# Inputs laid out by feature on the host, and index queries in five interleaved parts

## The reference

```python
def dsa_mixer(x, cos, sin, w_in, w_o):
    proj = x @ w_in
    q, k, v, iq, ik, iw = jnp.split(proj, A_SPLITS, axis=-1)
    ...
    s = jnp.einsum('bqhd,bsd->bqhs', iq_b, ik) * IDX_DIM ** -0.5
    score = jnp.einsum('bqh,bqhs->bqs', iw_b, jax.nn.relu(s))
    _, sel = lax.top_k(score, top_k)
...
    x = layer_norm_2(DEEPNORM_ALPHA * x + swiglu_ffn(x, ffn_w_in[i], ffn_w_down[i]), ...)
    x = x + jax.nn.sigmoid(x @ ple_w_gate[i]) * (p[i] @ ple_w_proj[i])
```

## Time and profile before

| | us |
|---|---|
| median of 3 runs | 1242.28 |
| lowest and highest run | 1242.15 and 1244.17 |
| span of the profiled execution | 1239.5 |
| PE busy in it | 1229.5 |
| DVE busy | 853.1 |
| ACT busy | 589.4 |

### The profile page before, as it was taken

How to read it: one execution, slowest core, us unless ns; L and a number is a source line. 1 busy time by engine, 2 the same in 40 slices (tenths; PEclk the granted TensorE clock), 3 DMA queues, 4 the chain that set the end, 5 groups by cost and what they waited for, 6 DMA issues and landing times.

```text
span 1239.5 us, 18755 instructions
## 1 busy us (share of the span) xinstructions
PE 1229.5 (99%) x7999; PEld 1050.9 (85%) x7999; DVE 853.1 (69%) x919; ACT 589.4 (48%) x712; POOL 94.9 (8%) x226
## 2 busy tenths in 40 slices
PE   9999999999999999999999999999999999999998
PEld 8888888888888888888988888888898888888887
DVE  6887776665775776666776676668587666766675
ACT  5774444334754544334654444345472544444434
POOL 5441000001000200000101000001000100000000
PEclk9999999999999999999999999999999999999999
DMA  8425665655633755654615656555564347655642
GB/s 282 170 69 166 209 197 181 199 187 156 221 115 129 266 183 191 202 175 157 222 60 182 216 181 203 180 194 204 180 191 158 103 150 237 200 186 188 200 141 101
DMA packets 127234, 221.03 MB, mean 178 GB/s; under 512 B 7048, under 2 KB 91296, under 8 KB 127152
## 3 DMA queue, kind: packets, MB, share of 16 engines
q1 hardware_dynamic: 124128, 209.83, 51.0%
q0 software_dynamic: 3024, 10.01, 2.6%
HBM read 218.77 MB, written 1.05 MB: 177 GB/s over the span
## 4 chain that ended last, share of the span: by engine, by line
PE 93%; DVE 3%; ACT 2%; DMA 1%; POOL 1%; issue 1%; SPq 0%; POOLq 0%; DVEq 0%
PE ps L794 20%; PE ps L622 18%; PE ps L796 10%; PE ps L599 10%; PE ps L600 10%; PE ps L601 10%; PE ps L762 4%; PE ps L810 2%; PE ps L706 2%; DVE wlo L1870 1%; PE ps L1034 1%; PE ps L981 1%; DMA raw<-in_ffn_w_in 1%; PE ps L1149 1%; ACT whi L1421 1%
## 5 line engine op out<-in xcount | busy, mean ns | idle before, releaser
L1870 DVE TENSOR_TENSOR wlo<-raw,whi 128x2048 fp32r<-128x2048 f32 (+3 forms) x203 | 452.1, 2241 | 174.6 <-ACT whi L1421 173.4
L1421 ACT ACTIVATE whi<-raw 128x2048 fp32r<-128x2048 f32 (+3 forms) x203 | 376.8, 1869 | 73.0 <-DMA raw<-in_hgrn_w_in 21.7
L794 PE MATMUL ps<-xhl,whi 128*128 128x512 f32 x1088 | 271.8, 392 | 0.0
L794 PEld LDWEIGHTS ps<-xhl,whi 128*128 128x128 f32 x1088 | 198.4, 188 | 37.4
L622 PE MATMUL ps<-whi,xhl 128*128 128x512 f32 (+1 forms) x736 | 182.6, 380 | 0.7 <-ACT xhl L1438 0.6
L599 PE MATMUL ps<-whi,hh 128*128 128x512 f32 x432 | 168.8, 391 | 0.0
L600 PE MATMUL ps<-whi,hl 128*128 128x512 f32 x432 | 168.6, 390 | 0.0
L601 PE MATMUL ps<-wlo,hh 128*128 128x512 f32 x432 | 168.1, 389 | 0.0
L796 PEld LDWEIGHTS ps<-xhl,wlo 128*128 128x128 f32 x1088 | 148.4, 190 | 10.6
L622 PEld LDWEIGHTS ps<-whi,xhl 128*128 128x128 f32 x736 | 130.7, 188 | 26.0 <-issue 0.9
L796 PE MATMUL ps<-xhl,wlo 128*128 128x256 f32 x1088 | 151.7, 282 | 0.0
(11 more groups left out here) (342 smaller groups left out, 1354.8 us busy)
## 6 DMA issues: line engine op xcount, KB each, us to landing
raw<-in_ffn_w_in SPq DMA_DIRECT2D x40, 1024.0 KB, 5.1
raw<-in_mlp_w_up SPq DMA_DIRECT2D x32, 1024.0 KB, 5.4
raw<-in_mlp_w_down SPq DMA_DIRECT2D x32, 1024.0 KB, 4.9
raw<-in_ffn_w_down SPq DMA_DIRECT2D x22, 1024.0 KB, 4.8
raw<-in_hgrn_w_in SPq DMA_DIRECT2D x16, 1024.0 KB, 6.0
raw<-in_b_w_in SPq DMA_DIRECT2D x12, 1024.0 KB, 5.6
raw<-in_ple_w_gate SPq DMA_DIRECT2D x8, 1024.0 KB, 6.0
raw<-in_a_w_in SPq DMA_DIRECT2D x6, 1024.0 KB, 5.8
```

The lines of the kernel that those rows point to most:

```text
L794: mm(bank(b + f), w[0][:, kk, P * f : P * f + P], xhl[:, kk, :, :].rearrange("p a n -> p (a n)"), start=(kk == 0), stop=False)
L1421: a.activation(whi[:, slot, 0:w], raw[:, slot, 0:w], ACT.Copy).then_inc(s["hi_done"], 1)
L1870: v.tensor_tensor(wlo[:, slot, 0:w], raw[:, slot, 0:w], whi[:, slot, 0:w].bitcast(F32), ALU.subtract).then_inc(s["lo_done"], 1)
```

## The change

The host lays out four inputs anew, without arithmetic: `x_columns` is x with features on the partitions, `position_columns` both position vectors with four numbers for each partition, `vector_columns` the 24 rows of the small vectors as columns, `side_columns` p with features on the partitions.

The index queries come in five parts of 1, 1, 2, 2 and 2 feature blocks, so there is one chunk more (204). SP issues for each part first x's features (into `xT`, which lies in the place of `y`) and then its weights. ACT makes, part by part, the high part of x and then that of the weights, DVE the low parts in the same order. PE turns the identity 14 times and then multiplies the five parts with both token tiles inside. Sixteen transposes of x, 14 fillers and the transpose of `vrow` with its copy go. POOL issues one load for the positions and one for the vectors, straight to `vcol`. x by token, which only the first layer norm reads, is loaded ahead of the fourth `dsa_q` chunk. The side input is loaded by feature, and ACT and DVE split it from SBUF; its 4 transposes in each of two layers go, and with them PE's waits for the load and for the bank.

Left out of the diff: the numbering of the turns without the first one, semaphores that go with what goes, the second side input's load (as the first), and the waits for `vcol` that become waits for its load.

```diff
--- before.py
+++ after.py
@@ -90,6 +90,7 @@
+        xT = nc.alloc_sbuf_tensor_at("xT", [P, KD, SEQ], F32, offset=y_home)
...
@@ -158,8 +158,9 @@
-        for q in range(4):
-            chunk("dsa_iq", rows_of(a_in, 2 * q, 2, A_IQ, 512), 2, 512)
+        IQ_PARTS = [(0, 1), (1, 1), (2, 2), (4, 2), (6, 2)]
+        for k0, kn in IQ_PARTS:
+            chunk("dsa_iq", rows_of(a_in, k0, kn, A_IQ, 512), kn, 512)
...
@@ -241,12 +242,15 @@
             def load_x(tt):
-                sp.dma_start(x[:, tt, :], t["x"][0, tt * P : (tt + 1) * P, :]).then_inc(s[f"x_landed{tt}"], 16)
...
-            load_x(0)
+                sp.dma_start(x[:, tt, :], t["x"][0, tt * P : (tt + 1) * P, :]).then_inc(s["x_landed"], 16)
...
-                if n == 1:
-                    load_x(1)
+                if n < len(IQ_PARTS):
+                    k0, kn = IQ_PARTS[n]
+                    sp.dma_start(xT[:, k0 : k0 + kn, :], t["x_columns"][:, k0 : k0 + kn, :]).then_inc(s[f"xT_landed{n}"], 16)
+                if n == first["dsa_q"] + 3:
+                    for tt in range(TT):
+                        load_x(tt)
...
@@ -398,12 +402,8 @@
-            for w, name in enumerate(("positions", "positions_2")):
-                pool.dma_start(posi[:, w, :], t[name][0].rearrange("(t p) -> p t", p=P), allow_slow_non_contiguous=True).then_inc(s["pos_landed"], 16)
-            pool.dma_start(vrow[V_BA : V_BA + 4, :], t["b_b_a"][0].rearrange("(r p) -> r p", p=P)).then_inc(s["vrow_landed"], 16)
-            pool.dma_start(vrow[V_QN : V_QN + 2, :], t["mla_q_norm_2"][0].rearrange("(r p) -> r p", p=P)).then_inc(s["vrow_landed"], 16)
-            pool.dma_start(vrow[V_KVN : V_KVN + 2, :], t["mla_kv_norm_2"][0].rearrange("(r p) -> r p", p=P)).then_inc(s["vrow_landed"], 16)
-            pool.dma_start(vrow[V_LB : V_LB + 16, :], t["hgrn_lb_logits_2"].rearrange("l (h p) -> (l h) p", p=P)).then_inc(s["vrow_landed"], 16)
+            pool.dma_start(posi[:, :, :], t["position_columns"]).then_inc(s["pos_landed"], 16)
+            pool.dma_start(vcol[:, :], t["vector_columns"]).then_inc(s["vcol_landed"], 16)
@@ -564,7 +564,7 @@
-            pool.dma_start(ptok, t["p_2"][0, 0].rearrange("(t p) d -> p t d", p=P)).then_inc(s["p_landed"], 16)
+            pool.dma_start(sideT, t["side_columns"][0]).then_inc(s["p_landed"], 16)
...
@@ -843,13 +839,6 @@
-                pe.wait_ge(s["p_landed"], 16 * (layer + 1))
-                pe.wait_ge(s["rows_out"], 2 * ROWS_AT[(T_X5, T_X8)[layer]] + 1)
-                for tt in range(TT):
-                    for q in range(2):
-                        last = nc.tensor.transpose(ps[:, 0, 256 * q + P * tt : 256 * q + P * tt + P], ptok[:, tt, P * q : P * q + P], ident[:, :])
-                last.then_inc(s["p_turned"], 1)
@@ -1018,35 +1007,26 @@
-            def index_queries(q, tiles, parts):
...
+            def index_queries(q):
...
+                k0, kn = IQ_PARTS[q]
-                w = weights(n, 2, 512)
-                for part, w_part in parts:
+                w = weights(n, kn, 512)
+                for part, w_part in ((0, 0), (1, 0), (0, 1)):
...
+                        pe.wait_ge(s["xT_lo" if part else "xT_hi"], q + 1)
-                    for tt in tiles:
-                        for kk in range(2):
-                            if kk == 0 and q % 2 == 0 and not w_part:
-                                pe.wait_ge(s["turn_lo" if part else "turn_hi"], 2 * tt + q // 2 + 1)
-                            last = mm(bank(2 + tt), (xh, xl)[part][:, 2 * q + kk, P * tt : P * tt + P], w[w_part][:, kk, :],
-                                      start=(q == 0 and (part, w_part) == (0, 0) and kk == 0), stop=(q == 3 and w_part == 1 and kk == 1))
-                return last
...
-            HI, LOW_X, LOW_W = (0, 0), (1, 0), (0, 1)
-            keep_fed(12)
-            turn_tile(T_X0, x, 0)
-            keep_fed(16)
-            index_queries(0, [0], [HI, LOW_X])
-            turn_tile(T_X0, x, 1)
-            index_queries(0, [0], [LOW_W])
-            index_queries(0, [1], [HI, LOW_X, LOW_W]).then_inc(s["w_done"], 1)
-            for q in range(1, 4):
-                index_queries(q, range(TT), [HI, LOW_X, LOW_W]).then_inc(s["w_done"], 1)
-            pe.wait_ge(s["vrow_landed"], 64)
-            nc.tensor.transpose(ps[:, 6, 0:V_ROWS], vrow[:, :], ident[0:V_ROWS, 0:V_ROWS]).then_inc(s["vrow_turned"], 1)
+                    for kk in range(kn):
+                        for tt in range(TT):
+                            last = mm(bank(2 + tt), (xh, xl)[part][:, k0 + kk, P * tt : P * tt + P], w[w_part][:, kk, :],
+                                      start=(k0 + kk == 0 and (part, w_part) == (0, 0)), stop=(k0 + kk == KD - 1 and w_part == 1))
+                last.then_inc(s["w_done"], 1)
...
+            keep_fed(14)
+            for q in range(len(IQ_PARTS)):
+                index_queries(q)
...
@@ -1507,8 +1486,8 @@
                     if g == 0:
-                        act.wait_ge(s["p_turned"], layer + 1)
-                        a.activation(hh[:, P_SLOT, :], bank(0), ACT.Copy).then_inc(s["p_hi"], 1)
+                        act.wait_ge(s["p_landed"], 16 * (layer + 1))
+                        a.activation(hh[:, P_SLOT, :], sideT, ACT.Copy).then_inc(s["p_hi"], 1)
@@ -1622,16 +1601,17 @@
-            turned_tile(T_X0, 0)
-            until(first["dsa_iq"])
-            turned_tile(T_X0, 1)
+            for q, (k0, kn) in enumerate(IQ_PARTS):
+                act.wait_ge(s[f"xT_landed{q}"], 16)
+                a.activation(xh[:, k0 : k0 + kn, :], xT[:, k0 : k0 + kn, :], ACT.Copy).then_inc(s["xT_hi"], 1)
+                until(first["dsa_iq"] + q)
...
-            act.wait_ge(s["w_done"], first["dsa_iq"] + 4)
+            act.wait_ge(s["w_done"], first["dsa_iq"] + len(IQ_PARTS))
...
@@ -1922,6 +1903,8 @@
+                if i == 0:
+                    dve.wait_ge(s["x_landed"], 16 * TT)
@@ -1990,7 +1973,7 @@
-                        v.tensor_tensor(hl[:, P_SLOT, :], bank(0), hh[:, P_SLOT, :].bitcast(F32), ALU.subtract).then_inc(s["p_lo"], 1)
+                        v.tensor_tensor(hl[:, P_SLOT, :], sideT, hh[:, P_SLOT, :].bitcast(F32), ALU.subtract).then_inc(s["p_lo"], 1)
@@ -2161,12 +2144,12 @@
-            turned(T_X0, 0)
-            until(first["dsa_iq"])
-            turned(T_X0, 1)
-            until(first["dsa_iq"] + 3)
...
-            dve.wait_ge(s["pos_landed"], 32)
+            for q, (k0, kn) in enumerate(IQ_PARTS):
+                dve.wait_ge(s["xT_hi"], q + 1)
+                v.tensor_tensor(xl[:, k0 : k0 + kn, :], xT[:, k0 : k0 + kn, :], xh[:, k0 : k0 + kn, :].bitcast(F32), ALU.subtract).then_inc(s["xT_lo"], 1)
+                until(first["dsa_iq"] + q)
...
+            dve.wait_ge(s["pos_landed"], 16)
...
@@ -2495,11 +2475,23 @@
...
+def laid_out(inputs):
...
+    arrays = {name: np.asarray(inputs[name]) for name in INS}
+    arrays["x_columns"] = np.asarray(inputs["x"])[0].reshape(SEQ, KD, P).transpose(2, 1, 0)
+    arrays["position_columns"] = np.stack([np.asarray(inputs[name])[0].reshape(TT, P).T for name in ("positions", "positions_2")], axis=1)
+    rows = [np.asarray(inputs[name]).reshape(-1, P) for name in ("b_b_a", "mla_q_norm_2", "mla_kv_norm_2", "hgrn_lb_logits_2")]
+    arrays["vector_columns"] = np.concatenate(rows).T
+    side = np.asarray(inputs["p_2"])[:, 0]
+    arrays["side_columns"] = side.reshape(DEPTH, SEQ, 2, P).transpose(0, 3, 2, 1).reshape(DEPTH, P, 2 * SEQ)
+    return {name: np.ascontiguousarray(a) for name, a in arrays.items()}
 def kernel(**inputs):
```

33 lines of the change are left out of this document (12 added, 21 removed).

## The result

The changed kernel takes 1246.32 us (median of 5 runs, 1244.39 to 1246.95), the kernel before took 1242.15 beside it (1241.54 to 1244.17): ratio 1.0027, 95% interval 1.0016 to 1.0038. It is slower by 4.2 us, where I had forecast 1240.4. The profiled execution has a span of 1244.9 us and a time of 1246.9, so the time lies 2.0 us above the span.

What follows compares the result with a forecast made beforehand. The prediction took PE's matmul side, busy 1229.5 of 1239.5 us, as the bound. Gains of 1.0 us at the start and 0.9 at the side input made 1242.3 - 1.9 = 1240.4 us, range 1238.5 to 1242.8 us.

Steps and rivals of the forecast that it cites:

- First matmul at 5.0 us: Start of PE: first index-query matmul at 5.0 us in place of 8.09, 3 us of head start.
- Last weights at 12.8 us, 13.4 at worst: Last index-query weights land at 12.8 us if half the 1.3 us hole goes; bounds 12.1 and 13.4.
- the hole: DMA flow of 133 GB/s between 6.5 and 8.5 us, beside GpSimd's small loads; said to cost 1.3 us.
- the bytes ahead of the last weights are the same: Start's DMA: still 1 MB of x and 2 MB of weights, in ten transfers in place of six.
- my first rival: The hole in the DMA closes: last weights land at 12.1 us, gain 2.6, time 1239.7 us; chance 0.20.
- Short transfers: A rule against five parts at the start: ten shorter transfers would flow slower, last weights landing no sooner than before.
- my third case: Front of the DMA comes no sooner: landing at 13.4 us, gain 1.3, time 1241.0 us; chance 0.16.
- dsa_k at landing + 9.7 us, with PE waiting about 2 us: DVE's work after the landing gates dsa_k: start at 22.5 us for 23.5, gain 1.0, bounds 0.4 and 1.7.
- Side input 0.9 us, bounds 0.7 and 0.9: Side input in two layers: four transposes and a slower matmul group behind them go, 0.45 us each.
- 39 matmuls fewer, x by token, `vrow`, new waits at no cost: PE loses 39 matmuls; x's later load, the vrow transpose and the new waits count 0 us.
- Carry-through: After 23.5 us PE runs dense and its releasers move with it, so the early 1.0 us is kept whole.
- PE's clock stays low: Rival at the start: index-query matmuls take 0.454 us for 0.227; 1247.6 us, milder form 1242.8; chance 0.09.

Runs made afterwards that it cites:

- before_noposition: The kernel before without the load of its two position vectors (angles made from zeros): 1242.82 us, ratio 1.0003.
- parts4: The changed kernel with the index queries in four parts of two feature blocks in place of five parts: ratio 1.0023 to the kernel before.
- the dense runs: Runs of the changed kernel with each part's x pieces side by side in DRAM, alone or with further edits: ratios 0.9973 to 1.0013 to the kernel before.
- xdense: The changed kernel with each part's x pieces side by side in DRAM, steps of 2 KB in place of 8 KB: ratio 1.0013 to the kernel before.
- dense4_late: The changed kernel with four parts, x pieces side by side in DRAM and two weight transfers (chunks 57 and 159) issued later: 1239.45 us, ratio 0.9974.
- parts4_pad30: The changed kernel with four parts of two blocks and 30 more identity turns on PE: 1243.77 us, ratio 1.0011 to the kernel before.
- pad30: The changed kernel with 30 more identity turns on PE, 20 ahead of the second part and 10 ahead of dsa_k: ratio 0.9998 to the kernel before.
- delay2: The changed kernel with two weight transfers (chunks 58 and 160) issued later, PE's instructions untouched: 1241.38 us, ratio 0.9986 to the kernel before.
- delay: The changed kernel with two weight transfers (chunks 58 and 162) issued later, PE's instructions untouched: 1243.51 us, ratio 1.0009 to the kernel before.

## Why the forecast was wrong, step by step

- **First matmul at 5.0 us.** Right: 5.21 us.
- **Last weights at 12.8 us, 13.4 at worst.** Wrong: 14.52 us. Half of the step stood up: the hole was the small pieces of the positions (before_noposition). The failed half is "the bytes ahead of the last weights are the same", by which I let the new transfers flow like the old ones. Two costs were missing. Five parts in place of four cost 1.0 us (parts4, pieces of 1 KB included; 0.6 to 1.1 among the dense runs), and x by feature in steps of 8 KB costs 1.3 us (xdense; 0.9 to 1.4 among the runs with four parts, 13.36 to 13.52 against 12.08 to 12.47; 1.0 to 2.0 among those with five). Without both, the landing is 12.19 us (dense4_late), which is the closed hole of my first rival. Why the step of the addresses costs that, no run tells.
- **Short transfers.** The rows first: ten transfers gave 223 GB/s from 2.5 to 6.5 us, eight gave 254 (parts4, where x's pieces of 1 KB go too); with the new step it was 277 and 353. The Trainium skill, DMA: Bandwidth & Descriptors, section Bandwidth, gives short transfers less bandwidth than long ones; the trace agrees with its direction. This was my third case, and I had given it 0.16 and a landing no later than 13.4 us, as if shorter transfers could only take back what the hole gave.
- **dsa_k at landing + 9.7 us, with PE waiting about 2 us.** Right: 14.52 + 9.62 = 24.14 us, and PE waits 1.40 us for DVE. It is 9.62 to 9.64 us in all seven kernels where PE is there first (12.08 to 14.52 us), and 0.2 to 0.5 us more in the others, parts4_pad30 apart, as there PE is late (a part ran at the lower clock, below) and DVE's copy of the queries waits for it. So the start costs 0.6 us, where I had a gain of 1.0.
- **Side input 0.9 us, bounds 0.7 and 0.9.** Right: 0.45 us each in the changed kernel; 0.5 each alone in the kernel before.
- **39 matmuls fewer, x by token, `vrow`, new waits at no cost.** Right; no wait at the first layer norm or at the fourth `dsa_q` chunk.
- **Carry-through, "the gain whole".** This is the step that made the sign. I took what happens after 23.5 us to be a matter of semaphores alone, since PE's rows are dense there. But in the kernel before the code's packet and a weight transfer already met at 329.3 us with nothing to spare: PE came to the new block 1.6 us behind the packet's end, at the second place 1.2 us. The change takes 62 of PE's instructions away ahead of the edge (31 matmuls and their weight loads, not the 79 that I wrote ahead of pad30), so the edge falls later in the program, 0.53 us behind the issue of the weight transfer where it was 0.27, and the packet came behind the transfer: 2.22 + 1.47 + 1.91 = 5.6 us, by the table. Without it (delay2) the changed kernel is 1.3 us faster than before by the medians, with a start that is still late: the forecast's sign, and two thirds of its 1.9 us. That is in part luck: its `dsa_k` comes at 24.41 us, 0.9 us late, which takes the side input's 0.9 back, and on the profiled executions nothing is left. The kernel before can meet standstills that delay2 can't (its runs spread from 1241.2 to 1244.4 us, those of delay2 from 1240.9 to 1242.0), and no run held the two transfers back in the kernel before, so what the change is worth without them isn't shown.
- **Clock.** The rival "PE's clock stays low" had the wrong place. At the start the first part stepped by 0.26 us a matmul. The lower level came at 335.4 us, behind a standstill that no case of mine held. The rival is not empty, though: in delay and delay2, whose instructions on PE are those of the changed kernel, PE idled 2.6 and 2.8 us ahead of the third part, whose first 8 matmuls then took 3.46 and 3.01 us in place of 2.06, and `dsa_k` came 0.3 us later than in the changed kernel.

The sum on the profiled executions: +0.6 (start) + 5.6 (code) - 0.9 (side input) = +5.3 of the 5.4 us; 0.1 drifts in between. By medians it is 4.2 us. The profiled run of the changed kernel was 0.6 us above its median. That of the kernel before was a good one: the listed runs take 1.7 to 2.0 us more than their spans, so with a span of 1239.5 it took 1241.2 to 1241.5 us, 0.6 to 1.7 us less than the medians of its runs (1242.15 to 1242.94), and not the 2.8 us of the forecast's sum. A span set against a span is thus good for finding the place of a loss, and the ratio for its size: delay2's span is 0.5 us longer than that of before, while its median is 1.3 us shorter.

Open: why, of the packets whose transfer starts at the same moment (below), some go at once and some wait; what costs the 1.3 us near 670 us; and whether the first stretch of the changed kernel's flow has a third cause, as dense x with five parts has 277 GB/s and with four 353.

## What to carry to other kernels

Ask of every edit that changes the count or the timing of instructions on a dense engine where its code is fetched: look for "issue" waits in bursts of short instructions, count in steps of 256 instructions from one of them, and look at what large transfer was issued just ahead of the edge one block earlier; holding back two transfers that had slack gave more here than padding did (1241.4 against 1242.5 us). When a transfer is re-laid or cut, price its flow anew, by the number of transfers and by the step between its pieces in DRAM, even where the bytes are the same. And where two chains end together, as ahead of `dsa_k`, a gain on one is worth nothing until the other is shortened too.
